# A two-layer encoder trunk: other sums of squares, roots and gating order at three transitions between sub-layers

## The reference, cut to what matters

```python
for i in range(DEPTH):
    sh_t, sc_t, g_t, sh_c, sc_c, g_c = jnp.split(silu(c) @ ada_w[i] + ada_b[i], 6, axis=-1)
    h = mixer(rms_norm(x, norm_g[i, 0]) * (1 + sc_t) + sh_t)      # S5, or attention
    x = x + g_t * rms_norm(h, norm_g[i, 1])
    h = rms_norm(x, norm_g[i, 2]) * (1 + sc_c) + sh_c
    h = conv_ffn(h, ...)
    x = x + g_c * rms_norm(h, norm_g[i, 3])
```

## Time and profile before

| | |
|---|---|
| median of 3 executions | 1278.6 us (1278.41 to 1278.99) |
| the profiled execution's own time | 1281.96 us |
| its span, first to last instruction | 1280.2 us |
| PE busy | 1222.6 us (96%) |
| DVE busy | 769.1 us (60%) |
| ACT busy | 530.5 us (41%) |
| POOL busy | 393.8 us (31%) |
| mean granted TensorE clock | 0.981 |

### The profile page before, as it was taken

The page is one execution under the profiler, slowest core; times in us unless marked ns, Lnnn a source line. Parts: engine busy times, 40 slices in busy tenths (PEclk is TensorE's granted clock), DMA queues, the critical chain, the costliest instruction groups (busy, mean ns, idle before and its releaser), DMA issues.

```text
span 1280.2 us, 17797 instructions
## 1 busy us (share of the span) xinstructions
PE 1222.6 (96%) x6527; PEld 984.5 (77%) x6527; DVE 769.1 (60%) x1065; ACT 530.5 (41%) x813; POOL 393.8 (31%) x265
## 2 busy tenths in 40 slices
PE   4978999999999999999999999998999999999997
PEld 2756888678888887888788777676788888887886
DVE  8879587868975444242873678857754444443225
ACT  3283444343344443141432567765344444432211
POOL 4961100245644334000112554600243333441000
PEclk9998999889999999999899999998899999999999
DMA  7957645244753223323123232211022222223221
GB/s 277 359 184 221 235 162 201 93 165 174 289 193 104 94 98 104 108 97 119 46 99 115 67 100 82 66 67 66 33 99 98 98 98 98 98 99 109 93 94 66
DMA packets 26697, 162.21 MB, mean 127 GB/s; under 512 B 4496, under 2 KB 4816, under 8 KB 8400
## 3 DMA queue, kind: packets, MB, share of 16 engines
q1 hardware_dynamic: 25632, 161.15, 35.8%
q10 hardware_dynamic: 1008, 0.28, 0.1%
HBM read 152.76 MB, written 2.10 MB: 121 GB/s over the span
## 4 chain that ended last, share of the span: by engine, by line
PE 82%; DVE 8%; issue 4%; DMA 3%; ACT 2%; SPq 1%; ACTq 0%; DVEq 0%; POOL 0%
PE psum L1852 17%; PE psum L1854 16%; PE psum L1853 16%; PE psum L1948 3%; PE psum L1950 3%; PE psum L1949 3%; PE psum L2041 3%; PE psum L2043 3%; PE psum L2042 3%; PE psum L1729 2%; DMA ada_raw<-in_ada_w 1%; PE psum L2099 1%; PE psum L1694 1%; PE psum L2084 1%; PE psum L2086 1%
## 5 line engine op out<-in xcount | busy, mean ns | idle before, releaser
L1852 PE MATMUL psum<-hhi,whi 128*128 128x512 f32 x960 | 381.1, 397 | 4.8 <-DVE wlo L1267 3.4
L1853 PE MATMUL psum<-hlo,whi 128*128 128x512 f32 x960 | 375.1, 391 | 0.0
L1854 PE MATMUL psum<-hhi,wlo 128*128 128x512 f32 x960 | 375.1, 391 | 0.0
L1267 DVE TENSOR_TENSOR wlo<-raw,whi 128x2048 fp32r<-128x2048 f32 x81 | 193.5, 2388 | 176.2 <-ACT whi L717 176.2
L717 ACT ACTIVATE whi<-raw 128x2048 fp32r<-128x2048 f32 x80 | 153.1, 1914 | 165.7 <-PE psum L2043 76.4
L555 POOL TENSOR_TENSOR ca<-ca,cb 128x512 f32<-128x512 f32 x44 | 144.1, 3275 | 239.8 <-ACT ca L841 239.8
L1852 PEld LDWEIGHTS psum<-hhi,whi 128*128 128x128 f32 x960 | 180.8, 188 | 47.9 <-DVE wlo L1267 4.8
L1854 PEld LDWEIGHTS psum<-hhi,wlo 128*128 128x128 f32 x960 | 180.9, 188 | 38.4
L1853 PEld LDWEIGHTS psum<-hlo,whi 128*128 128x128 f32 x960 | 181.1, 189 | 35.6
L1434 DVE SCALAR_TENSOR_TENSOR ca<-psum,convp,ca 128x511 f32<-128x511 f32 x44 | 33.0, 749 | 211.6 <-ACT ca L837 211.6
L843 ACT ACTIVATE ghi<-ca 128x512 f32 (+1 forms) x44 | 27.8, 632 | 157.0 <-POOL ca L555 157.0
(11 more groups left out here) (356 smaller groups left out, 1882.5 us busy)
## 6 DMA issues: line engine op xcount, KB each, us to landing
raw<-in_units SPq DMA_DIRECT2D x92, 1024.0 KB, 4.8
ada_raw<-in_ada_w SPq DMA_DIRECT2D x24, 1024.0 KB, 7.6
ada_ring<-in_ada_w SPq DMA_DIRECT2D x24, 1024.0 KB, 4.8
qk_sw<-ca SPq DMA_DIRECT2D x32, 128.0 KB, 2.3
u<-in_x_blocks SPq DMA_DIRECT2D x1, 2048.0 KB, 7.6
x<-in_x_t SPq DMA_DIRECT2D x1, 2048.0 KB, 8.5
out_rows<-y_late SPq DMA_DIRECT2D x8, 256.0 KB, 2.1
bc_par<-in_s_bc SPq DMA_DIRECT2D x1, 1024.0 KB, 5.6
```

The costliest lines, as they stand in the source:

```text
L1267: TT(wlo[:, s, :], raw[:, s, :], whi[:, s, :].bitcast(F32), ALU.subtract).then_inc(split_lo, 1)
L1852: M(out, w_hi, hi[:, k, :], start=(k == 0), stop=False)
L1853: M(out, w_hi, lo[:, k, :], start=False, stop=False)
L1854: return M(out, w_lo, hi[:, k, :], start=False, stop=(k == KT - 1))
```

## The change

It has four parts.

1. The squares of the last tiles are not added by DVE. `DIRECT_A` and `DIRECT_C` name the tiles of each transition: for a the last one in r = 0 and 1 and the last two in r = 2; for c the last two in r = 2. PE sums them over the partitions straight from `sq` and `ca`, in further groups of four products that accumulate into the same PSUM columns. The sum of the first tiles is taken as soon as it is ready. The idle products are counted and placed anew: 7, 6, 6 and 12 become 0, 4, 7 and 14 in r = 1; r = 0 has 4 between the two groups of a; in r = 2, 7, 2, 2 and 12 become 5, 2, 2 and 14.
2. `root_of` takes 10 instructions in place of 12, counted with the addition of eps: one longer polynomial step of four instructions and a shorter one of three. The root over the input near the start keeps the Newton steps.
3. In r = 0 ACT makes the gated y right after the first square, and squares that, in place of squaring with the gate first.
4. In r = 0 DVE copies the sums of x squared out of PSUM before the last unit of the projection, no longer at the head of `both_roots`.

```diff
--- before.py
+++ after.py
@@ -342,6 +342,11 @@
             return layer, 24 * ffn
 
 
+        DIRECT_A, DIRECT_C = ((7,), (7,), (6, 7)), ((), (), (6, 7))
+
+        def sum_count(direct, r, f):
+            return sum(KT - 1 - len(d) for d in direct[:r]) + min(f, KT - 1 - len(direct[r]))
+
         POOL_CL = (5, 6, 7, 8)
 
         block = ctx.enter_context(nc.Block())
@@ -754,10 +759,11 @@
                 act.wait_ge(y_ready, f + 1)
                 wait(act, sum_a, f - 2 if f > 2 else 0)
                 A(sq[:, f % 2, :] if f else ssum[:], y, ACT.Square).then_inc(sqa_ready, 1)
+                act.wait_ge(sqa_ready, f + 1)
+                A(y, y, ACT.Copy, scale=g).then_inc(yg_ready, 1)
+                act.wait_ge(yg_ready, f + 1)
                 wait(act, sum_c, f - 2 if f > 2 else 0)
-                A(glu_sq[:, f % 2, :] if f else cb[:, 1, :], y, ACT.Square, scale=g).then_inc(sqc_ready, 1)
-                act.wait_ge(sqc_ready, f + 1)
-                A(y, y, ACT.Copy, scale=g).then_inc(yg_ready, 1)
+                A(glu_sq[:, f % 2, :] if f else cb[:, 1, :], y, ACT.Square).then_inc(sqc_ready, 1)
 
             def glu(i, s):
                 act.wait_ge(unit_done, i + 1)
@@ -805,10 +811,10 @@
 
                 y, g = psum[:, y_bank(r, f), :], gate[:, r, f:f + 1]
                 wait_y(act, r, f)
-                wait(act, sum_a, 7 * r + f - 2 if f > 2 else 0)
+                wait(act, sum_a, sum_count(DIRECT_A, r, f - 2) if f > 2 else 0)
                 A(sq[:, f % 2, :] if f else ssum[:], y, ACT.Square).then_inc(sqa_ready, 1)
                 A(y_late[:, f, :], y, ACT.Copy, scale=g).then_inc(yg_ready, 1)
-                wait(act, sum_c, 7 * r + f - 2 if f > 2 else 0)
+                wait(act, sum_c, sum_count(DIRECT_C, r, f - 2) if f > 2 else 0)
                 A(ca[:, f % 2, :] if f else cb[:, 1, :], y, ACT.Square, scale=g).then_inc(sqc_ready, 1)
 
             def spread_first(r):
@@ -1054,18 +1060,28 @@
             def rsqrt(dst, src, scale, lk, op=ALU.mult, t=None):
 
                 w = dst.shape[1]
-                v, t = nwt[:, 0, 0:w], nwt[:, 1, 0:w] if t is None else t
+                newton = t is not None
+                v, t = nwt[:, 0, 0:w], t if newton else nwt[:, 1, 0:w]
                 lk(TS(v, src, scale, EPS, op, ALU.add))
-                root_of(dst, v, t, lk)
-
-            def root_of(dst, v, t, lk):
+                root_of(dst, v, t, lk, newton)
+
+            def root_of(dst, v, t, lk, newton=False):
 
                 lk(TS(t.bitcast(I32), v.bitcast(I32), 1, None, ALU.logical_shift_right))
                 lk(TS(dst.bitcast(I32), t.bitcast(I32), -1.0, RSQRT_MAGIC, ALU.mult, ALU.add))
-                for i in range(3):
-                    lk(TT(t, dst, dst, ALU.mult))
-                    lk(STT(t, t, -0.5, v, ALU.mult, ALU.mult))
-                    lk(STT(dst, t, 1.5, dst, ALU.add, ALU.mult))
+                if newton:
+                    for i in range(3):
+                        lk(TT(t, dst, dst, ALU.mult))
+                        lk(STT(t, t, -0.5, v, ALU.mult, ALU.mult))
+                        lk(STT(dst, t, 1.5, dst, ALU.add, ALU.mult))
+                    return
+                lk(TT(t, dst, dst, ALU.mult))
+                lk(TT(t, t, v, ALU.mult))
+                lk(STT(t, t, -10.0 / 3.0, t, ALU.add, ALU.mult))
+                lk(STT(dst, t, 5.0, dst, ALU.add, ALU.mult))
+                lk(TT(t, dst, dst, ALU.mult))
+                lk(STT(t, t, -27.0 / 1024.0, v, ALU.mult, ALU.mult))
+                lk(STT(dst, t, 0.5625, dst, ALU.add, ALU.mult))
 
             def reduced(dst_sin, dst_cos, ang, t, lk):
 
@@ -1355,9 +1371,9 @@
 
                 n = KT * r + f + 1
                 y, sqc = (y_late, ca) if r else (y_glu, glu_sq)
-                if f:
+                if f and f not in DIRECT_A[r]:
                     dve.wait_ge(sqa_ready, n)
-                    wait(dve, sum_a, 7 * r + f - 1)
+                    wait(dve, sum_a, sum_count(DIRECT_A, r, f - 1))
                     TT(ssum[:], ssum[:], sq[:, f % 2, :], ALU.add).then_inc(sum_a, 1)
                 dve.wait_ge(yg_ready, n)
                 if r:
@@ -1368,15 +1384,13 @@
                     dve.wait_ge(sum_b, KT * r + f)
                     link(TT(bx, x[:, f, :], y[:, f, :], ALU.mult))
                     TT(cb[:, 0, :], cb[:, 0, :], bx, ALU.add).then_inc(sum_b, 1)
+                if f and f not in DIRECT_C[r]:
                     dve.wait_ge(sqc_ready, n)
-                    wait(dve, sum_c, 7 * r + f - 1)
+                    wait(dve, sum_c, sum_count(DIRECT_C, r, f - 1))
                     TT(cb[:, 1, :], cb[:, 1, :], sqc[:, f % 2, :], ALU.add).then_inc(sum_c, 1)
 
             def both_roots(r):
 
-                if r == 0:
-                    dve.wait_ge(stat_x, 1)
-                    link(nc.vector.tensor_copy(stat[:, 24:24 + QT], psum[:, 5, 0:QT]))
                 dve.wait_ge(stat_a, r + 1)
                 r1, r2, mean = stat[:, 16:16 + QT], stat[:, 20:20 + QT], stat[:, 24:24 + QT]
                 rsqrt(r1, psum[:, 4, 0:QT], 1.0, link)
@@ -1527,6 +1541,8 @@
                 glu(i, i % 2)
             first_half_low(0)
             ada_step(N_GLU - 1, 1, 4, N_GLU - 1, 0)
+            dve.wait_ge(stat_x, 1)
+            link(nc.vector.tensor_copy(stat[:, 24:24 + QT], psum[:, 5, 0:QT]))
             glu(N_GLU - 1, 1)
             next_input(0, {KT - 1: lambda: second_half_low(0)})
             dve.wait_ge(h_low, KT)
@@ -1909,35 +1925,53 @@
 
             def barrier(r):
 
+                sqc = ca if r else glu_sq
+                n_a, n_c = sum_count(DIRECT_A, r, KT - 1), sum_count(DIRECT_C, r, KT - 1)
+
+                def over_features(bank, c0, tile, start, stop):
+                    for t in range(QT):
+                        ins = M(psum[:, bank, c0 + t:c0 + t + 1], tile[:, P * t:P * t + P], col[:, 0:1],
+                                start=(start and t == 0), stop=stop, skip_group_check=True)
+                    return ins
+
                 pe.wait_ge(split_lo, (U_FIN[0], U_V, U_FIN[1])[r] + 1)
-                idle_products(7, 7)
-                pe.wait_ge(sum_a, 7 * r + 7)
-                for t in range(QT):
-                    ins = M(psum[:, 4, t:t + 1], ssum[:, P * t:P * t + P], col[:, 0:1], start=True, stop=True)
+                if r == 2:
+                    idle_products(5, 7)
+                pe.wait_ge(sum_a, n_a)
+                over_features(4, 0, ssum, True, False)
+                if r == 0:
+                    idle_products(4, 7)
+                for f in DIRECT_A[r]:
+                    pe.wait_ge(sqa_ready, KT * r + f + 1)
+                    ins = over_features(4, 0, sq[:, f % 2, :], False, f == KT - 1)
                 ins.then_inc(stat_a, 1)
+                if DIRECT_C[r]:
+                    pe.wait_ge(sum_c, n_c)
+                    over_features(6, QT, cb[:, 1, :], True, False)
+                    for f in DIRECT_C[r]:
+                        pe.wait_ge(sqc_ready, KT * r + f + 1)
+                        over_features(6, QT, sqc[:, f % 2, :], False, f == KT - 1)
                 pe.wait_ge(sum_b, KT * r + KT)
-                for t in range(QT):
-                    M(psum[:, 6, t:t + 1], cb[:, 0, P * t:P * t + P], col[:, 0:1], start=True, stop=True)
-                pe.wait_ge(sum_c, 7 * r + 7)
-                for t in range(QT):
-                    ins = M(psum[:, 6, QT + t:QT + t + 1], cb[:, 1, P * t:P * t + P], col[:, 0:1],
-                            start=True, stop=True)
+                ins = over_features(6, 0, cb[:, 0, :], not DIRECT_C[r], True)
+                if not DIRECT_C[r]:
+                    pe.wait_ge(sum_c, n_c)
+                    ins = over_features(6, QT, cb[:, 1, :], False, True)
                 ins.then_inc(stat_c, 1)
                 if r == 2:
                     broadcast_gate(0, 3)
                 else:
-                    idle_products(6, 3)
+                    idle_products(4, 3)
                 pe.wait_ge(spread1, r + 1)
                 M(psum[:, 5, :], ones[:], diag[:].rearrange("p t s -> p (t s)"), start=True,
                   stop=True).then_inc(row1_psum, 1)
                 if r == 2:
                     broadcast_gate(1, 2)
                 else:
-                    idle_products(6, 3)
+                    idle_products(7, 3)
                 pe.wait_ge(spread2, r + 1)
                 M(psum[:, 7, :], ones[:], on[:].rearrange("p t s -> p (t s)"), start=True,
                   stop=True).then_inc(row2_psum, 1)
-                idle_products(12, 0 if r == 2 else 3)
+                idle_products(14, 0 if r == 2 else 3)
                 if r == 2:
                     pe.wait_ge(row_copied, 8)
 
```

## The result

The changed kernel takes 1272.38 us, the median of 5 runs (1270.43 to 1273.38), against 1278.99 for the kernel before on the same chip (1278.41 to 1281.79). The ratio is 0.994 (95% interval 0.9928 to 0.9953): 6.6 us, or 0.6%, faster. The forecast was 1275.2 with a range of 1273.0 to 1277.9. The sign was right, and the gain was almost twice the forecast's 3.4, outside the range. Over all runs made here the changed kernel's mean is 1272.8 (22 times, standard deviation 1.1) and that of before 1279.2 (the 115 times beside e1 to e16, 2.0; all 131 give 1279.3), so 6.4 us.

What follows compares the result with a forecast made beforehand. The prediction took TensorE's own list, with its idle products and the half clock, to bound the kernel. Gains of 0.75 + 0.6 + 0.95 + 0.4 + 0.7 = 3.4 us gave 1275.2 us, range 1273.0 to 1277.9.

Steps and rivals of the forecast that it cites:

- What bounds the kernel: Whole kernel: TensorE carries 82% of the chain, so an edit gains only where TensorE's own list advances earlier.
- Transition 0: From the gated y to r2's spread: earlier gated y, fewer slow idle products, r2 out at 241.9 against 242.66; gain 0.75 us.
- Transition 1: One DVE addition fewer and earlier wide work: gain 0.9 us at one end, loss 0.3 at the other, 0.6 taken.
- the bad end: Transition 1: the clock falls before the group on b, both last groups take 1.71 each; a loss of 0.3 us.
- The roots: Two instructions fewer per root, 0.19 us each: hidden by PE's list in the transitions, gain 0.4 at the kernel's end.
- The stretch after transition 0: Half clock near 272, 6.75 us long, keeps its shape or shortens to 3.35; gain 0 to 1.7 us, 0.7 taken.
- Transition 2: DVE loses four additions, PE runs seven groups in place of three; r2 out at 904.0 against 904.95, gain 0.95 us.
- 2.7/1.05 = 2.6 groups fit: Transition 2: groups of small sums that run at full clock, 1.05 us each, before the clock falls at 889.3.
- clock back at 902.3: Transition 2: full clock returns at 902.3, by the taken 5.5 us of wide work before a return.
- Given back: Rival, chance 0.27: wide work starts earlier in each transition but the clock returns no earlier; gain 0.75 us, 1277.9.
- Larger: Rival, chance 0.17: every end at its good side, including the short low stretch at 272; gain 5.55 us, 1273.1.
- Slower: Rival, chance 0.08: seven small groups at half clock and a clock that stays low over 8 us; +3.2 us, 1281.8.

Runs made afterwards that it cites:

- e1: The kernel before with only transition 2's direct sums and idle products changed, roots and other transitions as before: 1276.05 us, ratio 0.9973.
- e16: The changed kernel with more idle products where PE waits, six ahead in transition 2, timed a second time: mean of its 12 times 1271.4 us.
- e7_noidle2: The changed kernel without the five idle products ahead of transition 2's sums: 1276.53 us, ratio 0.9984 to the kernel before.
- e4_t0: The kernel before with only transition 0's part of the change: 1279.03 us, ratio 0.9998.
- e3_roots: The kernel before with only the ten-instruction roots: 1278.03 us, ratio 0.9991.
- e5_t1: The kernel before with only transition 1's part of the change: 1279.10 us, ratio 1.0003.
- e2_not_t2: The changed kernel with transition 2's sums and idle products as in the kernel before: 1276.18 us, ratio 0.9972.
- e13_newton: The changed kernel with the old twelve-instruction roots: 1274.01 us in 6 runs, ratio 0.9966 to the kernel before.
- e9: The changed kernel with fewer idle products behind the sums, and none ahead of transition 2's gate rows; the text gives no measured time.
- e11: The changed kernel with more idle products where PE waits and fewer between sums, r1 and r2 in transitions 0 and 1; no measured time given.
- e8: The changed kernel with transition 2's c squares of tiles 6 and 7 added by DVE again: 1275.24 us, ratio 0.997 to the kernel before.
- e10: The changed kernel with more idle products where PE waits, six ahead in transition 2: mean of 12 times, over two occasions, 1271.4 us.
- e14: The changed kernel with two idle products between each two of transition 2's first six groups of small sums: 1277.24 us, ratio 0.9986 to the kernel before.
- e17: The changed kernel with more idle products where PE waits, nine ahead in transition 2: that transition 16.2 us, times of 1274.3 and 1275.1 remain.
- e18: The changed kernel with fewer idle products behind transitions 0 and 1's sums, four behind their direct sums, nine ahead in transition 2: not at 1271.5 us.

## Why the prediction was off

*What bounds the kernel* held: behind the first sums the chain lies on PE's own list in all transitions. That an edit gains by letting this list advance is only half of it, since five products taken out ahead of the sums made the kernel 3.7 us slower (e7_noidle2).

*Transition 0*, forecast 0.75: 0.75 in the first trace, 0.8 in e4_t0. The price of each step was right too, the copy and ACT's order included. That it hit exactly is luck: S0 moves by 1 us between executions of the changed kernel.

*Transition 1*, forecast 0.6: 0.54, with two errors that cancel, which is luck too. The fall before the last groups, which I had priced as the bad end, came true (616.45, one pair at 3.57). But wide work began at 620.04 and the clock was back at 623.25, after 3.2 us and not my 5.5.

*The roots*, forecast 0.4 at the end and nothing elsewhere: 0.38, and nothing in e3_roots' other segments.

*The stretch after transition 0*, forecast 0.7 between 0 and 1.7: 1.5 in the first trace, but 0 and 2.8 in the next two, the last beyond its good end. The mean of the three is 1.4. It follows from the execution, and a 0.7 was as good as a row could give.

*Transition 2* is the step that failed: forecast 0.95, at most 1.45, and 4.2 in three profiles (3.2 ± 1.9 by e1_t2's times). "From 886.6" was right (1.5 us after the products). Two terms were mis-sized. "2.7/1.05 = 2.6 groups fit" counts a group at full clock at 1.05, which is its length to the end of its last product; the next group starts 0.91 after it. With 0.91, 3.0 groups would run fast and 4.0 slow, 2.7 + 6.8 = 9.5 us for the forecast's 10.2: 0.7 us. And "clock back at 902.3", 5.5 us after wide work begins, came 892.90 - 889.57 = 3.3 us after it, which is worth 1.0. So even with the fall where the forecast had it, the term should have been 0.95 + 0.7 + 1.0 = 2.65. e1_t2, with its fall at 4.1 us for the forecast's 4.3, measured 2.6 in its one profile.

The third part is the fall's place, which was read from one trace of before. In after it came 6.0 us after the products and not 4.3, so (886.10 - 881.57)/0.91 = 5.0 groups ran fast and two slow, 8.0 us for 9.5: the other 1.5. PE was busy for 5.83 of those 6.03 us, where in before it stood idle from 886.8 to 892.75. But that this moved the fall is not shown: with PE mostly idle the old list too had it at 6.1 and 6.2 us in two profiles (e5_t1, e2_not_t2), and the busy new list had it at 3.3 in one (e13_newton). What is shown is that the new list's gain hangs on it. That the fall could move stood in my own rivals, but only in the bad direction.

Two of the forecast's sums don't come out of its own rows, without weight for the result. With the clock back at 901.7, transition 2's good end is 1.25 and not 1.45; and half way between 1275.2 and 1277.9 is 1276.5, not 1276.9.

The Trainium skill's formula for a load, 128 columns over 1.2 or 107 ns, has no term for the clock ("TensorE: Matmul & The Clock Gate", "LDWEIGHTS (loading the stationary operand)"). The forecast's estimate by it, 4 us for transition 2, is near the 4.2 measured, but the trace contradicts its reason: the seven groups took 8.0 us and not 6.0. With 6.0 the forecast's own steps would give some 5 (896.8 - 892.6 = 4.2 more than 0.95), not 4. The loads of PE in this stretch (minimum, median and maximum in ns), first at full and then at half clock:

```profile
L1933 PEld LDWEIGHTS psum<-col,sq x16: 192/192/192, 882.5 to 884.1; 128*128 128x128 f32 x16
...
L1933 PEld LDWEIGHTS psum<-col,cb x8: 333/333/333, 887.7 to 889.1; 128*128 128x128 f32 x8
```

The clock does matter to them, by 1.7 times, and the same seven groups take 10.5 us in e13_newton, with the early fall, against 8.0 in after.

*The rivals.* Given back did not occur. Larger had each part at its good side and came nearest, but it too bounded transition 2 at 1.45. Slower, by seven groups at half clock, is what e7_noidle2 almost builds (10.97 of 12.0), and even with it S2 is 19.0, 0.9 shorter than before. What it lacks is the half clock behind the sums: the clock is back at 899.18, 3.9 us after wide work begins, and the rival needed over 8.

What stays open is why the fall comes at 3.3 to 4.3 us after the products in some executions (before, e1, e3, e4, e9, e11, e13, e16) and at 5.8 to 6.7 in others (all three of the changed kernel, e2, e5, e8, e10, e14), with the old list or the new. With nine idle products ahead (e17, e18) it came at 6.8 and 7.3, in one profile each, and with none (e7) at 2.8. That the changed kernel nearly always has the late fall is likely from its narrow times (1.1 against 2.0), but not shown. Nor is it settled whether the roots' 1.2 us in the means (e3_roots, e13_newton) are more than the trace's 0.4.

## What to carry to other kernels

When a change fills or empties the time ahead of a fall of the clock, don't take the fall's place from the trace of before: price the work behind it once with the fall early and once late, and keep both in the range. A short gap of the engine that bounds, filled with a few wide products, can be worth three times their length. Here it was so ahead of the small work, where the engine would have waited (e7_noidle2), and not between the small work, where it would not (e14_between2). Cut two profiles at common marks before comparing them, take the same mark in each (the end of the last real product, whether or not idle ones follow), and take three profiles of a kernel when a clock decides.

## What the runs showed of the hardware

A group of four single-column sums in float32 costs 0.91 us at full clock and 1.71 at half, nearly the whole factor of two, though its products have one column. The low stretches in all 20 profiles were 3.4, 6.8, 10.2 or 13.6 us long, but for the one that each kernel ends in. Those lengths don't follow the kernel's list alone: with the same seven groups in front, transition 2's lasted 6.8 us in after and 13.65 in e13_newton, and after transition 0 the changed kernel had 3.4, 6.8 and none. With 6.8, 3.4 and none of it F took 375.8, 374.2 and 372.9 us, so 3.4 us less of half clock was worth 1.3 to 1.5 there. The clock makes most of the spread of one kernel's times. Of the 126 executions of before that were timed beside the experiments, 69 had a mean granted clock of 0.979 to 0.982 and took 1280.5 us in the mean; 20 had 0.986 to 0.990 and took 1275.9.
